# Attention values by features, two heads side by side in the array, in a two-block transformer kernel on one core

## The reference

```python
qkv = u @ w_in[i]
q_a, k_a, v_a, q_b, k_b, v_b = jnp.split(...)
o_a = stick_breaking_attention(...)   # A[t,s] = beta_ts * prod_{s<j<t}(1 - beta_tj), s < t
o_b = chunk_band_attention(...)       # softmax(q k^T + relative bias), block-causal by chunks of 64
mixed = jnp.concatenate([rms_norm_2(merge_heads(o_a), g_out_sb[i]),
                         rms_norm_2(merge_heads(o_b), g_out_ch[i])], axis=-1)
h = h + rms_norm_2(mixed @ w_out[i], g_mix_post[i])
```

## Time and profile before

| | us |
|---|---|
| median of 3 runs | 968.76 |
| lowest and highest | 968.25, 969.23 |
| span of the profiled execution | 967.1 |
| PE busy, idle | 954.8, 12.3 |
| DVE, ACT, POOL busy | 703.0, 490.7, 53.3 |

### The profile page before, as it was taken

How to read it: one execution, slowest core, us unless ns; L and a number is a source line. 1 busy time by engine, 2 the same in 40 slices (tenths; PEclk the granted TensorE clock), 3 DMA queues, 4 the chain that set the end, 5 groups by cost and what they waited for, 6 DMA issues and landing times.

```text
span 967.1 us, 14404 instructions
## 1 busy us (share of the span) xinstructions
PE 954.8 (99%) x5644; PEld 818.8 (85%) x5644; DVE 703.0 (73%) x912; ACT 490.7 (51%) x650; POOL 53.3 (6%) x90
## 2 busy tenths in 40 slices
PE   8999999999999999999999999999999999999997
PEld 5798788888988888889888888898988888888885
DVE  3589998579879999758776763474656977775455
ACT  3574565864465555325445433248855644444342
POOL 0241000000000000010000000001101000000000
PEclk9999999999999999999999999999999999999999
DMA  9954353665476655943665555173522565555511
GB/s 373 400 225 172 134 215 132 234 241 192 182 264 216 216 180 209 333 170 124 249 241 213 178 213 195 66 285 133 192 100 87 215 232 184 190 201 194 197 44 44
DMA packets 27987, 190.13 MB, mean 197 GB/s; under 512 B 3136, under 2 KB 3520, under 8 KB 5920
## 3 DMA queue, kind: packets, MB, share of 16 engines
q1 hardware_dynamic: 26336, 184.23, 51.6%
q0 software_dynamic: 1456, 5.12, 1.7%
q10 hardware_dynamic: 144, 0.07, 0.0%
HBM read 188.35 MB, written 1.05 MB: 196 GB/s over the span
## 4 chain that ended last, share of the span: by engine, by line
PE 92%; DMA 3%; ACT 2%; issue 1%; DVE 1%; SPq 0%; POOL 0%; POOLq 0%; DVEq 0%; ACTq 0%
PE acc L1160 23%; PE acc L1163 11%; PE acc L700 10%; PE acc L702 10%; PE acc L701 10%; PE acc L703 4%; PE acc L705 4%; PE acc L704 4%; DMA early<-in_early 3%; PE acc L847 3%; PE acc L1104 2%; PE acc L1032 1%; PE acc L1011 1%; PE acc L1135 1%; PE acc L1107 1%
## 5 line engine op out<-in xcount | busy, mean ns | idle before, releaser
L1943 DVE TENSOR_TENSOR wlo<-raw,whi 128x2048 fp32r<-128x2048 f32 (+1 forms) x140 | 316.3, 2266 | 141.7 <-ACT whi L1443 141.6
L1443 ACT CAST whi<-raw 128x2048 fp32r<-128x2048 f32 (+1 forms) x144 | 270.4, 1889 | 141.3 <-PE acc L702 92.9
L1160 PE MATMUL acc<-x_parts,whi 128*128 128x512 f32 x960 | 301.5, 395 | 0.0
L1163 PEld LDWEIGHTS acc<-x_parts,wlo 128*128 128x128 f32 x960 | 180.3, 188 | 42.6
L1163 PE MATMUL acc<-x_parts,wlo 128*128 128x256 f32 x960 | 188.6, 278 | 0.0
L1160 PEld LDWEIGHTS acc<-x_parts,whi 128*128 128x128 f32 x960 | 146.1, 189 | 0.0
L700 PE MATMUL acc<-whi,h_hi 128*128 128x512 f32 x264 | 103.0, 390 | 0.0
L702 PE MATMUL acc<-whi,h_lo 128*128 128x512 f32 x264 | 102.7, 389 | 0.0
L701 PE MATMUL acc<-wlo,h_hi 128*128 128x512 f32 x264 | 102.7, 389 | 0.0
L703 PE MATMUL acc<-x_parts,whi 128*128 128x256 f32 x312 | 90.3, 289 | 0.0
L705 PE MATMUL acc<-x_parts,wlo 128*128 128x256 f32 x312 | 88.3, 283 | 0.0
(11 more groups left out here) (314 smaller groups left out, 1200.2 us busy)
## 6 DMA issues: line engine op xcount, KB each, us to landing
raw<-in_stream SPq DMA_DIRECT2D x164, 1024.0 KB, 4.8
early<-in_early SPq DMA_DIRECT2D x8, 1024.0 KB, 15.1
X<-in_x SPq DMA_DIRECT2D x2, 512.0 KB, 4.6
G<-in_ctx SPq DMA_DIRECT2D x1, 1024.0 KB, 22.0
bc<-in_g_ffn_post POOLq DMA_DIRECT2D x2, 512.0 KB, 4.9
MX<-in_bias POOLq DMA_DIRECT2D x1, 1024.0 KB, 6.4
out<-X SPq DMA_DIRECT2D x4, 256.0 KB, 2.1
bc<-in_c_row POOLq DMA_DIRECT2D x1, 512.0 KB, 4.7
```

The costliest lines, as they stand in the source:

```text
L1160: pe.matmul(acc[:, BANK[i + q] + o, :], w[0][:, k, o * P:(o + 1) * P], xs[:, k, :], start=(k == 0), stop=False)
L1163: mm = pe.matmul(acc[:, BANK[i + q] + o, T:2 * T], w[1][:, k, o * P:(o + 1) * P], xhi[:, k, :], start=False, stop=(k == KD - 1))
L1443: act.copy(of_split(whi[si_slot], si), of_split(raw[raw_slot], si)).then_inc(s["hi_done"], 1)
L1943: dve.tensor_tensor(of_split(wlo[slot], si), of_split(raw[raw_slot], si), of_split(whi[slot], si), ALU.subtract).then_inc(s["lo_done"], 1)
```

## The change

The values are computed by features. The values of a head, [128 keys x 64 features], are the stationary operand and the probabilities are the moving operand, 256 queries for the first key tile and 128 for the second. An even head writes PSUM partitions 0 to 63 and an odd one 64 to 127, that is, the two heads of a pair take the two halves of the array's columns. The result already has features in the partitions, so the transposes of `MX` go, and `MX` holds it in that layout.

What was a factor of a row is now one of a column, so two things move. The band probabilities are multiplied by the reciprocal of their row sum on POOL, before they are transposed. And for the norm, ACT squares the values (`stick_square`, `band_square`), DVE adds the squares of different features that lie in the same partition, PE sums over the partitions with a constant of 1/512 (`mix_sums`, `band_sums`, one column each), DVE adds epsilon, POOL takes the power, DVE puts the result on a diagonal (`mix_diagonal`) and PE multiplies that by a matrix of -1 to have it in all partitions (`mix_broadcast`). DVE then scales `MX` by gain and norm (`mix_scale`), and ACT and DVE make `xhi` and `xlo` from `MX`. The probabilities get four buffers instead of two.

```diff
+            mix_power(0)
+            for h in range(H2):
+                pool.wait_ge(s["b_rec"], h + 1)
+                for t, (lo, hi) in enumerate(((0, P), (P, SC))):
+                    at = band_p(h)[:, lo:hi]
+                    ins = pool.tensor_scalar(at, at, brec[:, 8 * t + h:8 * t + h + 1], None, ALU.mult)
+                ins.then_inc(s["b_scaled"], 1)
+            mix_power(1)
...
-                for h in range(GH):
-                    w, v = at(h), vv[:, :, (h0 + h) * HD2:(h0 + h + 1) * HD2]
...
+                for pair in range(GH // 2):
+                    heads = (2 * pair, 2 * pair + 1)
+                    for h in heads:
+                        at = (GH * g + h) * HD2
+                        pe.matmul(acc[HD2 * (h % 2):HD2 * (h % 2) + HD2, BANK[i], pair * T:(pair + 1) * T],
+                                  v2t[0][:, 0, at:at + HD2], sp4[:, h, 0:T], start=True, stop=False,
+                                  skip_group_check=True)
...
-            tiles_stage(SPLIT["kb0"], ACC["kb0"])
-            pe.wait_ge(s["a_ready"], 2)
...
+            def last_sticks():
+                pe.wait_ge(s["a_ready"], 2)
+                stick_values(1)
+
+            tiles_stage(SPLIT["kb0"], ACC["kb0"], between=last_sticks)
+            mix_sums()
...
                 for h in (2 * pair, 2 * pair + 1):
-                    pe.wait_ge(s["b_exp"], h + 1)
+                    pe.wait_ge(s["b_scaled"], h + 1)
...
-            tiles_stage(SPLIT["kb1"], ACC["kb1"])
-            transpose_tokens(5, MX, "mx_scaled", 0, range(KD // 2), MIX_BANKS)
+            tiles_stage(SPLIT["kb1"], ACC["kb1"], between=mix_broadcast)
...
                 mixed(pair // 2, 0, [(0, pair % 2), (1, pair % 2)])
-                band_values(pair)
                 if pair + 2 < H2 // 2:
                     band_scores(pair + 2)
+                band_values(pair)
...
+            stick_square(0)
             stick_ln(1)
...
+            band_copy(0)
+            band_copy(1)
+            band_exp(2)
+            band_exp(3)
+            band_square(0)
+            for pair in range(1, H2 // 2):
+                if pair < 3:
                     band_exp(2 * pair + 2)
+                band_copy(2 * pair)
+                band_copy(2 * pair + 1)
+                if pair < 3:
                     band_exp(2 * pair + 3)
...
+                band_square(pair)
+                if pair == 1:
+                    splits_to(SPLIT["wout2"] + 4)
...
-            splits_to(SPLIT["wout2"] + 2)
+            splits_to(SPLIT["wout2"] + 1)
             stick_out(1)
+            stick_sum()
...
+            mix_mean(0, "mixn")
+            splits_to(SPLIT["wout2"] + 2)
+            mix_diagonal(0)
             band_bias(0)
...
+            band_rec(0)
+            band_rec(1)
+            stick_parts()
+            band_bias(1)
             splits_to(SPLIT["wout2"] + 3)
...
             for pair in range(H2 // 2):
...
+                if pair < 3:
+                    band_rec(2 * pair + 2)
+                    if pair < 2:
+                        band_bias(pair + 2)
+                    band_rec(2 * pair + 3)
```

More of the change, by code:

```diff
@@ new lines, in mix_sums, with mix_broadcast @@
+            def mix_sums():
+                i = ACC["mixn"]
+                bank_free(i)
+                pe.wait_ge(s["mx_sum"], 2)
+                for t in range(TT):
+                    mm = pe.matmul(accb(i)[:, t:t + 1], sq_sum[:, t * P:(t + 1) * P], avg[:, 0:1], start=True, stop=True)
+                mm.then_inc(s["acc_ready"], 1)
+            def mix_broadcast(n=0):
+                i = ACC[("mixb", "bandb")[n]]
+                bank_free(i)
+                pe.wait_ge(s["mx_diag"], n + 1)
+                for t in range(TT):
+                    mm = pe.matmul(accb(i)[:, t * P:(t + 1) * P], negone, mix_diag[:, t * P:(t + 1) * P], start=True,
@@ L1837, in _ @@
             splits_to(SPLIT["wout2"] + 2)
+            stick_square(1)
             qk_out(3, "kb0", (0,))
@@ L1856, in _ @@
             qk_out(3, "kb1", (1,))
[L1857 to L1860, removed]
-                    if h >= 2:
-                        act.wait_ge(s["acc_ready"], ACC[f"band{pair - 1}"] + 1)
-                    act.copy(bt[:, h % 2, :], tp[:, 2 + h % 2, 0:SC]).then_inc(s["b_t"], 1)
-                if pair + 1 < H2 // 2:
+            for g in range(2):
+                act.wait_ge(s["mx_scaled"], 2 * g + 2)
+                act.copy(xhi[:, 2 * g:2 * g + 2, :], stick_t(g)).then_inc(s["xhi"], 1)
@@ new lines, in band_copy, with band_square @@
+            def band_copy(h):
+                act.wait_ge(s["b_tps"], h + 1)
+                if h >= 2:
+                    act.wait_ge(s["acc_ready"], ACC[f"band{h // 2 - 1}"] + 1)
+                act.copy(bt[:, h % 2, :], tp[:, 2 + h % 2, 0:SC]).then_inc(s["b_t"], 1)
+            def band_square(pair):
+                if pair == 0:
+                    bank_ready(ACC["mixn"])
+                act.wait_ge(s["band_o"], pair + 1)
+                act.activation(band_sqs[pair], band_t(pair), ACT.Square).then_inc(s["mix_sq"], 1)
@@ L1874, in _ @@
+            for n in range(4):
+                act.wait_ge(s["mx_scaled"], KD // 2 + n + 1)
+                act.copy(xhi[:, KD // 2 + n, :], band_t(n)).then_inc(s["xhi"], 1)
             splits_to(SPLIT["proj"] + 1)
@@ L2566, in band_out @@
-                chain(dve.reciprocal(r, sums))
                 bank_ready(i)
-                for t in range(TT):
-                    at = W2 + pair * P
-                    ins = dve.tensor_tensor(MX[:, t, at:at + P].rearrange("p (h d) -> p h d", h=2),
-                                            acc[:, BANK[i], t * P:(t + 1) * P].rearrange("p (h d) -> p h d", h=2),
-                                            r[:, t, :].rearrange("p (h d) -> p h d", d=1).broadcast_to([P, 2, HD2]),
-                                            ALU.mult)
```

201 lines of the change are left out of this document (125 added, 76 removed).

## The result

| | before | after |
|---|---|---|
| median of 4 runs (us) | 968.94 (968.25 to 969.23) | 978.80 (977.17 to 979.64) |
| profiled execution: time, span (us) | span 967.1 | 978.73, span 977.0 |
| PE busy, share of the chain that ended last | 954.8, 92% | 956.3, 88% |

The changed kernel is slower by a ratio of 1.0102 (95% interval 1.0090 to 1.0114). Forecast were 972.3 us and a range up to 976.4: the sign was right, the size was not, and the time lies outside the range.

The account below looks back on a forecast made before the run. TensorE, busy for 99% of the span, was taken as the bound. Waits of +7.3 us less 3.8 of shed work gave +3.5: span 970.6, with 1.7 around it 972.3 us; range 968.8 to 976.4.

Parts of the forecast that it names:

- waits: PE waiting on other engines' queues between the sticks and chunk 2: 7.8 us, less 0.5 already there, +7.3.
- GpSimd's 0.7 us a head: GpSimd's scaling of a head's 128 and 256 columns, taken as 0.3 + 0.4 us, bounds 0.4 and 1.7.
- PE's shed work: Stick and band values and MX transposes: 12.8 us removed from PE, 9.0 added, so 3.8 us less.
- Rival B: The two heads' streams don't overlap in stick groups and band pairs; 976.0 us, chance 0.05.
- Steps 1 and 2: Stick group 1 in kb0's middle waits 0.4 us; band scores 0 wait 0.4 for the copy of kb0's result.
- Step 3: First mixed products wait 0.6 us for x's low part; scores 2 then wait 0.3 for pair 1's bias.
- Step 4: Transposes of heads 2 and 3 wait 1.3 and 1.0 us behind VectorE's bias, split and reciprocals, and GpSimd's scaling.
- Step 5: Head 5 waits 1.1 us, its reciprocal being queued behind bias 6, 7, which wait for scores 3.
- Step 6: Values of pair 2 wait 1.8 us for ScalarE's copies; transposes of heads 6 and 7 wait 0.9.
- A: GpSimd is slow or held when scaling heads, 1.7 us a head; +7.0 in all, 975.8 us, chance 0.12.
- C: Not slower: VectorE does chunk 2's wlo split before PE reaches head 2's transposes; 966.2 us, chance 0.10.
- D: About level: two of four long waits absent as ScalarE or VectorE comes earlier; 968.8 us, chance 0.10.

Follow-up runs that it names:

- e3: Changed kernel with 26 unread products on PE ahead of the waits for scaled heads 2, 3, 5, 6 and 7; 976.05 us.
- e7: Changed kernel with three splits moved later in the VectorE and ScalarE queues and GpSimd scaling by a two-input product; 969.84 us.
- e8: Changed kernel with three splits moved later and no scaling of the probabilities, transposes waiting for the exponential; 970.18 us.
- e14: Whole change in a second queue layout: two-input scaling, reciprocals earlier, chunk 2 split in halves, chunk 3 split later, exponentials before squares; 968.88 us.
- e10: Changed kernel with GpSimd's scaling as a two-input product, queues as they were; 973.50 us.
- e11: Changed kernel with two-input scaling, VectorE's chunk 2 split early and chunk 3 split one pair later, ScalarE's queue reordered; 972.63 us.
- e9: Changed kernel with VectorE's wlo split of w_out chunk 2 moved ahead of the sticks' low parts and bias 2, 3; 980.47 us.
- e13: Changed kernel plus a one-input VectorE copy of 2048 columns beside GpSimd's scaling of heads 0 and 1; 979.67 us.
- e2: Changed kernel without GpSimd's scaling, transposes waiting for the exponential alone; 972.37 us.
- e4: Changed kernel with three splits moved later: VectorE's of chunk 2, ScalarE's and VectorE's of chunk 3; GpSimd unchanged; 972.12 us.
- e6: e4 with VectorE instead of GpSimd scaling the probabilities, right behind each reciprocal; 971.89 us.
- e1: Changed kernel without GpSimd's scaling, transposes waiting for VectorE's reciprocal; 971.90 us.

## Why the prediction was wrong

Three terms of the sum failed: the clock was put at nothing, the waits rested on GpSimd's 0.7 us a head, and PE's shed work was too large. Over the stretch, forecast +3.5 us, measured +9.6:

| term | forecast | measured | where |
|---|---|---|---|
| clock | 0 | +2.8 (2.3 to 2.8) | e3 |
| waits | 7.8 less 0.5 | +9.3 | waits of the changed kernel |
| PE's work | -3.8 | -2.5 (2.2 to 2.5) | e7, e8, e14 |

The 6.1 us between the two sums are 2.8 of clock, 2.0 of waits and 1.3 of work not shed.

**The clock** was left out. The prediction read a granted clock of 1.00 from the earlier trace rows and took it over into a stretch in which it put 7.8 us of idleness in front of PE. No step priced a fall: the largest failure. Whether waits of the forecast lengths alone would have brought it is open: e10, with 7.0 us of waits and none above 1.51, kept 1.00 in its profiled execution, and e11, with 5.6 us and one of 1.63, did not.

**PE's work.** The pieces were right or better: stick values 1.45 us a group (forecast 1.5), band values 0.80 a pair where both copies are there (0.9), six sums 1.3 (1.3), two broadcasts 0.7 (1.0). Rival B is out. What was missing is the joints, the places where small matmuls are put into a stream of products. Comparing timelines without waits, kb0's products take 6.06 us with the sticks in their middle instead of 5.80, kb1's 6.00 instead of 5.85, each of four groups of products 1.57 instead of 1.46 when scores or side-by-side values follow it, the last products 0.2 us more around the second sums and broadcast, and each of three pairs' transposes 0.2 us more than the idle time shown when a wait cuts into them. That is 1.7 us. And the 0.5 us of waiting that was to go did not: from the first transposes to the first product it was 0.88 us, and is 0.85 with the wait of 0.75 taken off.

**The waits**, by step. Steps 1 and 2 were exact: 0.42 (0.4) and 0.44 (0.4). Step 3 gave a wait of 0.75 for head 1 in place of 0.6 and 0.3: GpSimd's 1.5 us a head again. Step 4, heads 2 and 3: 2.06 and 0.93 (1.3, 1.0); the start of reciprocal 2, 717.39, was laid out at 716.8, the rest is GpSimd. Step 5, head 5: 1.67 (1.1). Step 6: 0.36 (1.8) for the values of pair 2, 1.51 and 1.17 (0.9) for heads 6 and 7. The mis-sized term is GpSimd's 0.7 us a head. The prediction had the right neighbour in hand, the one-input row of 0.70 for 128 columns (0.60 here), and went by the two-input row and the mask instead, without a reason against it. e7 shows that the choice was between the two forms: 0.97 is what the two-input form takes, so that 0.7 was too little even for it, and 1.50 the form that the kernel has.

**The rivals.** A (GpSimd at 1.7 a head, +7.0) was nearest: the rate is 1.5. But A's sum of waits was 11.3 us (7.8 + 3.5) where 9.3 came, and it was still 3 us short of the time, since it had no clock in it either. Its "held" half did not happen to the scalings of the changed kernel, where no split runs beside one, as the prediction said; e9 and e11 show that it is real. It did happen to a step that the prediction passed over: the small power of the sticks' norm took 2.69 us beside a split that started 0.17 us earlier (703.83), and 0.72 the second time, though PE did not wait for it:

```profile
704.00 2.69 POOL L703 TENSOR_TENSOR small<-small 128x2 f32<-128x2 f32 x1 [5.27 <-DVE small L2638]
...
741.02 0.72 POOL L703 TENSOR_TENSOR small<-small 128x2 f32<-128x2 f32 x1 [6.71 <-DVE small L2638]
```

The Trainium skill, GPSIMD Engine Reference, "Key points", says that GpSimd shares its SBUF interfaces with VectorE and contends with VectorE instructions "in a 2-port perf mode or with two SBUF inputs". e9 agrees with the second half (5.72 us instead of 3.02). The prediction and e13's theory used only that half. e13's copy has one input and held GpSimd too, which the first half allows, but no run here shows in which mode the copy ran. C was wrong in its mechanism: its condition was tried as e9 and costs 1.7 us, because the split then lies on GpSimd's scaling and a third fall of the clock comes with the earlier wait. D did not happen.

The range left out what no term allowed for. With A's upper bound for GpSimd and the slow clock twice it would have reached 978.6 (975.8 + 2.8), about the time measured, though with A's waits too long and the work shed too large.

## What to carry to other kernels

A wait put in front of a TensorE that was never idle can cost more than its length: price the lower clock behind it (here some 2.5 us on 9.3 us of waits), and allow for it in the range. The sum of the waits did not decide it: e2 had 4.6 us of waits and a fall, e4 5.5 us and none. When small matmuls are moved into streams of products, price the joints as well as the pieces. Take a GpSimd duration from a row of the same form, ask what VectorE does beside it, and where a fixed queue is the cover, lay out every queue again after each move: three of the moves here (e2, e6, e8) only passed the wait to the next engine.

## What the runs showed of the hardware

- GpSimd multiplies 128 and 256 f32 columns in place by a value per partition in 1.50 us as a one-input operation with a scalar, and in 0.97 us as a two-input product with the value broadcast.
- GpSimd stood still beside long VectorE instructions: four scalings of 3.02 us took 5.72 beside a 2.27 us subtraction and the two of x_parts behind it, and 4.82 with a 1.21 us one-input copy (0.9 us of it) and 1.29 us of subtractions (0.8). A power of 2 columns took 2.69 us beside a split and 0.72 without.
- In the profiled executions TensorE's granted clock went to the lower level behind waits of 2.06 and 0.93 us, 1.51 and 1.17, 1.63 and 0.83 (e11), and a single one of 2.60 (e2), but not behind 1.51 and 0.62 (e10) or a single one of 2.39 (e6). The runs give no simple line between them, and the mean clocks of e1 (0.999 or 0.996) and e10 (0.996 to 0.999) suggest that one program can fall on either side.
- Two heads' values side by side share their time only when both inputs are there: 0.80 us a pair, and 1.08 where the second head's copy came later (e8, 723.97 to 725.05).
